# Eight experts in five runs: two experts side by side in TensorE's array, and longer rows of weights

## The chip, the cores and the metric

The kernel runs on one core of one Trainium2 chip. The metric is the device time of one execution in microseconds (us); the lower the better. The time before is 1852.3 us, the median of three runs.

## What is computed

Two layers of a hybrid transformer over 256 tokens of width 1024, in 32-bit floats. The first layer has latent attention, an RWKV-7 recurrence and 32 small experts. The second has a pooling and convolution mixer, a dense feed-forward part, the mixer again, and then the part that the change is about: 8 experts of inner width 3584, of which each token uses two. In short:

```python
for e in range(8):
    hidden = silu(t @ w1[e]) * (t @ w3[e])       # w1, w3: 1024 x 3584
    y = y + combine[:, e:e + 1] * (hidden @ w2[e])  # w2: 3584 x 1024
```

After it come a layer norm and a gate of width 1024 times a small product, and the output is written. All weights are read from HBM once: 8 x 3 x 1024 x 3584 x 4 B = 352.3 MB for these experts.

## The kernel before, in words

The program is written out engine by engine: each engine has its own list of instructions, and semaphores order them. SP issues the DMAs of all weights into a ring of 7 places of 4096 floats per partition (2 MB each) and, for these experts, an eighth place in the space of the layer norms' parameters (`work`, in the trace `work<-in_exp_w`). The semaphore `used` counts pieces that TensorE has finished; SP waits on it before it overwrites a place (`expert_free`, line 575, and `pair_piece`, line 772, with its DMA at line 784).

The experts are sorted by how many tokens chose them. For each a number of slots is set aside: `WIDTHS` (line 514) has three groups, (128, 64, 64), (128, 64, 64) and (128, 32), filled with the experts of rank (0, 3, 4), (1, 5, 6) and (2, 7). Should an expert have more tokens than slots, a slow loop at the end does the rest; it isn't entered here. A group's work is cut into units of 1024 hidden columns, three of them and one of 512 (`PARTS`, line 517). `gather_wide`, `gather_narrow` and `gather_next` pick the tokens of the slots by a matmul with a selection matrix; `rows_of` (line 2113) multiplies by a piece of w1 or w3; `turn_wide` and `turn_narrow` transpose the hidden values, `down` (line 2150) multiplies by w2, and `group_scatter` and `last_scatter` bring the results back to the tokens, again by a matmul. On VectorE `product` (line 3061) multiplies SiLU(w1 part) by the w3 part, and `turned_copy` (line 3074) copies transposes from PSUM to SBUF; ScalarE computes SiLU (line 1265).

A wide expert (128 slots) fills TensorE's 128 columns. An expert of 64 slots uses half of them, so two halves of its own weight columns are multiplied at once, at two positions in the array (`tile_position`); one of 32 slots multiplies four quarters at once. The matmuls of wide experts stand at line 2127, those of narrow ones at line 2134; the down projections at 2168 and 2176. Within a unit the order is: wide w1, wide w3, narrow w1, wide transposes, narrow w3 (then the second narrow expert's w1 and w3), wide down, narrow transposes and down (`group_pe`, line 2103). In the last group the narrow expert's last two units come at the very end (`SCHEDULE`, line 554). A piece is 2 MB: of w1 and w3 four rows of 1024 columns (4096 B runs in HBM; 2048 B in the last unit), of w2 rows of 8192 B.

The first pieces of the first expert are sent before the router's result is known (`first`, line 786); the others wait for the semaphore step "over". After the last group SP loads the weights of the gate (line 821), and POOL the last norm's parameters (line 938).

Of the kernel before, what the change touches and what calls it, by code (L numbers as in the profile page):

```python
# [74 lines left out]
AHEAD = 7  # L75

# [101 lines left out]
def build(nc, x, positions, g_mix, w_in, g_cq, w_uq, g_ckv, w_uk, w_uv, g_qn, g_kn, g_mla_out, rw_mu, rw_w0, rw_w2,  # L178
# [4 lines left out]
    with ExitStack() as ctx:  # L183
# [150 lines left out]
        p_ga, p_sc, p_scT2 = cut(work, 0, TT, 2, P), cut(work, 512, TT, 2, P), cut(work, 1024, 2, TT, P)  # L334
        p_sw, p_swT, n2_hT = cut(work, 9760, TT, P), cut(c_sb[:, :, :].rearrange("p t n -> p (t n)"), 0, TT, P), cut(work, 9248, 4, P)

        def pair_x(widths):

            return cut(xT[:, :, :].rearrange("p k s -> p (k s)"), 0, KD, sum(widths))

        p_hs, p_hh, p_hT = cut(work, 1536, 2 * 512), cut(work, 2560, 2 * 512), cut(work, 3584, 8, P)
        p_yg, p_yn = cut(work, 4608, D), cut(work, 5632, D)
        n_hs, n_hh, n_hT = cut(work, 6656, 512), cut(work, 7168, 512), cut(work, 7680, 4, P)
# [3 lines left out]
        def rt(*shape):  # L347
# [15 lines left out]
        tables, at_rt = work, [8192]  # L363
# [3 lines left out]
        slot_of, comb_of = rt(2, E2 + 1), rt(2, E2 + 1)  # L367
        over_i = sb("over_i", [P, 1], I32)
        order_i = sb("order_i", [P, E2], I32)
# [45 lines left out]
        landed_x = sem("landed_x")  # L415
# [5 lines left out]
        w_silu, w_hid, w_hTd, w_hTs, n_silu, n_hid, n_hTd, n_hTs, p_sel, p_gath, p_xg, p_scT, p_turn, p_yg_s, p_scat, p_add = (  # L421
            sem(n) for n in ("w_silu", "w_hidden", "w_hT", "w_hTs", "n_silu", "n_hidden", "n_hT", "n_hTs", "p_sel", "p_gathered",
                             "p_xg", "p_scT", "p_turned", "p_yg", "p_scattered", "p_added"))
        p_sel_w, p_clear, p_y_last = sem("p_sel_w"), sem("p_clear"), sem("p_y_last")
# [79 lines left out]
        PLE1 = MOE0 + E2 * len(MOE)  # L504
# [5 lines left out]
        def read_moe(what, u):  # L510

            return MOE0 + MOE.index((what, u)) + 1
# [3 lines left out]
        GROUPS = len(WIDTHS)  # L516
        PARTS = [(f0, min(2 * 512, F2 - f0)) for f0 in range(0, F2, 2 * 512)]
        NU = len(PARTS)

        def members(p):  # L520
            return range(len(WIDTHS[p]))

        def in_order(p, m):

            return sum(len(WIDTHS[i]) for i in range(p)) + m

        def halves(u):
            return range(PARTS[u][1] // 512)

        def pieces_of(p):  # L530

            def of(m, u, *whats):
                return [(m, what, u, a) for what in whats for a in halves(u)]

            order = []
            for wide, narrow in SCHEDULE[p]:
                if (p, wide) == (0, 0):
                    order += of(0, 0, "w1", "w3") + of(1, 0, "w1") + of(0, 0, "w2") + of(1, 0, "w3")
                    order += of(2, 0, "w1", "w3") + of(1, 0, "w2") + of(2, 0, "w2")
                    continue  # L540
                if wide is not None:
                    order += of(0, wide, "w1", "w3")
                if narrow is not None:
                    for m in members(p)[1:]:
                        order += of(m, narrow, "w1", "w3")
                if wide is not None:
                    order += of(0, wide, "w2")
                if narrow is not None:
                    for m in members(p)[1:]:
                        order += of(m, narrow, "w2")  # L550
            return order

        together = [(u, u) for u in range(NU)]
        SCHEDULE = [together] * (GROUPS - 1) + [together[:2] + [(2, None), (3, None), (None, 2), (None, 3)]]
        SCATTER_AT, GATE_AT, PLE_AT = ((4, 5), (3, 7)), ((3, 7), (4, 5)), ((0, 1), (2, 6))

        PIECES = [pieces_of(p) for p in range(GROUPS)]
        assert sum(map(len, PIECES)) == E2 * len(MOE) and E2 * len(MOE) % (PLACES + 1) == 0

        def expert_slot(n):  # L560

            turn, at = divmod(n - MOE0, PLACES + 1)
            return (turn, None) if at == 1 else (turn, MOE0 + max(at - 1, 0))

        def expert_place(n):

            first = expert_slot(n)[1]
            return lnp.rearrange("p n d -> p (n d)") if first is None else place(first)

        def expert_landed(n):  # L570

            turn, first = expert_slot(n)
            return (landed_x, 16 * (turn + 1)) if first is None else (landed[(first + 1) % PLACES], 16 * (first // PLACES + 1 + turn))

        def expert_free(n):

            turn, first = expert_slot(n)
            if turn > 0:
                return used, n - PLACES
            return bl["dve"]("ln1 1 1") if first is None else (used, first - PLACES + 1)  # L580

        def piece_of(p, m, what, u, a):

            return MOE0 + sum(map(len, PIECES[:p])) + PIECES[p].index((m, what, u, a))

        def read_pair(p, m, what, u):

            return used, piece_of(p, m, what, u, halves(u)[-1]) + 1

        def narrow_count(p, m, u):  # L590

            return sum(NU * (len(WIDTHS[i]) - 1) for i in range(p)) + u * (len(WIDTHS[p]) - 1) + m

        def gathers(p):

            return 3 + 4 * p
# [12 lines left out]
        def _(sp):  # L609
# [162 lines left out]
            def pair_piece(n, at, what, u, a):  # L772
                f0, f = PARTS[u]
                dst = expert_place(n)
                if what == "w2":
                    src = exp_w2_2[0][at, f0 + a * 512:f0 + (a + 1) * 512, :]
                    src = src.rearrange("a (j p c) n -> p (a j) (c n)", j=2, p=P)
                    dst = dst.rearrange("p (j n) -> p j n", j=2)
                else:
                    src = (exp_w1_2 if what == "w1" else exp_w3_2)[0][at].rearrange("a (k p) f -> p (a k) f", p=P)  # L780
                    rows_k = PLACE // f
                    src = src[:, rows_k * a:rows_k * (a + 1), f0:f0 + f]
                    dst = dst.rearrange("p (k f) -> p k f", f=f)
                sp.dma_start(dst, src).then_inc(expert_landed(n)[0], 16)

            first = slice(0, 1)
            sent = [v for v in PIECES[0][:PLACES + 1] if v[0] == 0]
            for m, what, u, a in sorted(sent, key=lambda v: expert_slot(piece_of(0, *v))[1] is None):
                sp.wait_ge(*expert_free(piece_of(0, m, what, u, a)))
                pair_piece(piece_of(0, m, what, u, a), first, what, u, a)  # L790
            sp.wait_ge(*bl["dve"]("over"))
            for p in range(GROUPS):
                which = {0: first} if p == 0 else {}
                for m, what, u, a in PIECES[p]:
                    if p == 0 and (m, what, u, a) in sent:
                        continue
                    n = piece_of(p, m, what, u, a)
                    sp.wait_ge(*expert_free(n))
                    if m not in which:
                        at = in_order(p, m)  # L800
                        which[m] = ranked(order_i[0:1, at:at + 1])
                    pair_piece(n, which[m], what, u, a)

            extra2 = sp.value_load(over_i[0:1, 0:1], min_val=0, max_val=S // CAP2 - 1)
            with sp.If(extra2 > 0):

                with sp.Fori(E2, 2 * E2) as e:
                    at = ranked(order_i[0:1, bass.ds(e - E2, 1)])
                    for i, (what, u) in enumerate(MOE):
                        n = MOE0 + i  # L810
                        sp.wait_ge(used, e * len(MOE) + (n - PLACES + 1))
# [4 lines left out]
            for a in range(3):  # L816
                n = PLE1 + a
                sp.wait_ge(used, n - PLACES + 1)
                src = w_g[:, 4 * a - 4:4 * a, :] if a > 0 else ple_w_2[1].rearrange("(k p) n -> p k n", p=P)
                dst = place(n)[:, 0:src.shape[1] * D].rearrange("p (a b) -> p a b", b=D)  # L820
                sp.dma_start(dst, src).then_inc(ld_gate_w if a > 0 else ld_ple_w, 16)
# [8 lines left out]
        def _(pool):  # L830
# [98 lines left out]
            for l in range(L2):  # L929
# [14 lines left out]
        def _(act):  # L944
# [304 lines left out]
            def group_act(p):  # L1249
                widths = WIDTHS[p]  # L1250
                for wide, narrow in SCHEDULE[p]:
# [3 lines left out]
                    for m in members(p):  # L1255
                        u = narrow if m else wide
                        if u is None:
                            continue
# [1106 lines left out]
        def _(dve):  # L2365
# [780 lines left out]
            for j in (2, 3):  # L3146
                ins = dve.tensor_copy(p_yn[n * j:n * (j + 1), y * j:y * (j + 1)], ps[n * j:n * (j + 1), 6, 0:y])
                if j == 2:
                    link(ins)
# [92 lines left out]
```

## Time and profile before

| | us |
|---|---|
| median of 3 runs (1850.29 to 1853.62) | 1852.3 |
| the profiled execution, span from first to last instruction | 1847.9 |
| TensorE busy (matmuls) | 1727.2 |
| VectorE busy | 444.1 |
| ScalarE busy | 197.5 |
| DMA, queue q1 (SP's), share of 16 engines | 74.0% |

The page gives the span of the profiled execution and no other time of it. In the timeline a row is a stretch of like instructions of one line: its start and its length in us, engine, line, output and inputs, the shape and how many there were; [..] behind it is the idle time before, and what ended it. Some matmul records are missing, so counts can be a little low; each 32-bit matmul of the program is two instructions in the trace, a transpose is one. In the windows the last three numbers are the granted clock of TensorE (1.00 is full speed), the share of time in which the 16 DMA engines were busy, and GB/s.

### The profile page before, as it was taken

The page shows a single profiled execution, that of the slowest core. Times are in us where ns is not written, and L with a number is a line of the kernel's source. Part 1 is how long each engine was busy: PE and PEld are TensorE (multiplying, and loading weights), DVE is VectorE, ACT ScalarE, POOL GpSimd, SP SyncE. Part 2 cuts the span into 40 slices and gives each one's busy share as a digit, 9 for nine tenths or more (in the row PEclk, how much of TensorE's full clock was granted, in tenths as well). Part 3 has the DMA queues.
Part 4 walks back from the last instruction along what each step waited for, and adds up shares of the span by engine and source line. Part 5 has one row for each costly group of instructions (what it writes and reads, how often), then busy time and mean ns, then how long its engine had stood idle before and what let it go on. Part 6 is the DMA issues. An engine that isn't in the chain of part 4 may idle for free.

```text
span 1847.9 us, 21680 instructions
## 1 busy us (share of the span) xinstructions
PE 1727.2 (93%) x9492; PEld 914.1 (49%) x9492; DVE 444.1 (24%) x772; ACT 197.5 (11%) x332; POOL 40.4 (2%) x126
## 2 busy tenths in 40 slices
PE   8989997777999999999999999999999999999988
PEld 6679564343854444548563333354333334444443
DVE  2776531112632000037340010110101001100003
ACT  2352111111121000010210000000000000000011
POOL 4002000000000000000000000000000000000000
PEclk9999999899999999999999999999999999999999
DMA  7031659999665332452388999999999999999991
GB/s 278 4 137 73 252 240 421 422 422 405 233 237 182 137 137 68 147 205 67 141 318 337 409 417 409 417 397 409 417 409 417 409 417 397 411 413 414 408 394 41
DMA packets 136508, 548.24 MB, mean 297 GB/s; under 512 B 7585, under 2 KB 12818, under 8 KB 109282
## 3 DMA queue, kind: packets, MB, share of 16 engines
q1 hardware_dynamic: 133280, 540.67, 74.0%
q0 software_dynamic: 1664, 5.05, 0.8%
q8 instruction: 72, 1.18, 0.3%
q10 hardware_dynamic: 1474, 1.19, 0.2%
q14 instruction: 18, 0.15, 0.0%
HBM read 543.51 MB, written 1.05 MB: 295 GB/s over the span
## 4 chain that ended last, share of the span: by engine, by line
PE 74%; DMA 14%; DVE 6%; SPq 2%; ACT 1%; issue 1%; ACTq 0%; DVEq 0%
PE ps L2127 15%; PE ps L2134 10%; DMA ring<-in_w_down 7%; PE ps L2168 7%; DMA ring<-in_exp_w 6%; PE ps L2176 5%; PE ps L2010 4%; PE ps L1984 4%; PE ps L2025 4%; PE ps L1882 3%; PE ps L1835 3%; PE ps L1774 2%; PE ps L1954 2%; PE ps L1922 2%; PE ps L1665 1%; PE ps L1546 1%
## 5 line engine op out<-in xcount | busy, mean ns | idle before, releaser
L2127 PE MATMUL ps<-ring,xT 128*128 128x512 f32 x592 | 258.4, 594 | 3.5 <-DMA ring<-in_exp_w 2.6
L2134 PE MATMUL ps<-ring,xT 128*64 128x512 f32 (+3 forms) x1312 | 193.2, 480 | 3.1 <-DMA ring<-in_exp_w 3.1
L2127 PEld LDWEIGHTS ps<-ring,xT 128*128 128x128 f32 x592 | 111.3, 190 | 144.8 <-issue 138.9
L3072 DVE TENSOR_TENSOR work<-work,ps 128x512 f32<-128x512 f32 (+3 forms) x32 | 38.3, 1197 | 475.8 <-PE ps L2127 341.1
L2168 PE MATMUL ps<-ring,work 128*128 128x512 f32 x320 | 144.4, 609 | 8.0 <-DMA ring<-in_exp_w 4.5
L2134 PEld LDWEIGHTS ps<-ring,xT 128*64 128x64 f32 (+1 forms) x1312 | 73.5, 127 | 114.9 <-issue 97.4
L2168 PEld LDWEIGHTS ps<-ring,work 128*128 128x128 f32 x320 | 61.5, 195 | 87.0 <-issue 83.9
L2176 PE MATMUL ps<-ring,work 128*64 128x512 f32 (+1 forms) x576 | 96.2, 523 | 1.9 <-DVE work L3082 1.9
L1265 ACT ACTIVATE work<-ps 128x512 f32<-128x512 f32 (+3 forms) x32 | 21.1, 660 | 718.0 <-PE ps L2127 401.5
L1835 PE MATMUL ps<-xT,ring 128*128 128x256 f32 x384 | 86.3, 389 | 0.0
L1752 PE MATMUL ps<-ring,work 128*32 128x256 f32 x944 | 61.2, 414 | 20.4 <-DMA ring<-in_w_up 19.3
L1835 PEld LDWEIGHTS ps<-xT,ring 128*128 128x128 f32 x384 | 74.8, 195 | 10.7
L1984 PE MATMUL ps<-ring,work 128*128 128x512 f32 x176 | 77.6, 593 | 0.6 <-DVE work L2937 0.6
L2010 PE MATMUL ps<-ring,xT 128*128 128x512 f32 (+1 forms) x192 | 77.6, 557 | 0.2 <-ACT xT L1164 0.2
L2025 PE MATMUL ps<-ring,xT 128*128 128x512 f32 (+1 forms) x192 | 77.6, 557 | 0.0
L3082 DVE COPY work<-ps 128x512 f32<-128x512 f32 (+3 forms) x32 | 24.7, 771 | 207.0 <-PE ps L2147 157.2
L2176 PEld LDWEIGHTS ps<-ring,work 128*64 128x64 f32 (+1 forms) x576 | 32.5, 128 | 58.0 <-issue 50.7
L2879 DVE SCALAR_TENSOR_TENSOR work<-work,c_sb 128x256 f32<-128x256 f32 x120 | 58.2, 485 | 4.3
L1774 PE MATMUL ps<-ring,work 128*32 128x512 f32 x256 | 38.2, 748 | 22.0 <-DMA ring<-in_w_down 20.4
L2010 PEld LDWEIGHTS ps<-ring,xT 128*128 128x128 f32 x192 | 36.4, 190 | 40.0 <-issue 38.7
L1882 PE MATMUL ps<-ring,work 128*128 128x512 f32 x128 | 55.9, 592 | 0.0
L1752 PEld LDWEIGHTS ps<-ring,work 128*32 128x32 f32 x944 | 32.6, 118 | 46.7 <-DMA ring<-in_w_up 18.1
(540 smaller groups left out, 1674.2 us busy)
## 6 DMA issues: line engine op xcount, KB each, us to landing
ring<-in_exp_w SPq DMA_DIRECT2D x147, 2048.0 KB, 23.6
work<-in_exp_w SPq DMA_DIRECT2D x21, 2048.0 KB, 23.6
ring<-in_w_down SPq DMA_DIRECT2D x32, 1024.0 KB, 18.8
ring<-in_w_up SPq DMA_DIRECT2D x31, 1024.0 KB, 19.1
ring<-in_dense_w SPq DMA_DIRECT2D x15, 2048.0 KB, 8.1
ring<-in_w_gate SPq DMA_DIRECT2D x28, 1024.0 KB, 17.5
ring<-in_w_in SPq DMA_DIRECT2D x6, 2048.0 KB, 13.8
ring<-in_w_in SPq DMA_DIRECT2D x8, 1104.0 KB, 15.4
```

Source lines behind the costliest of these rows:

```text
L1752: ins = mm(ps[32 * j:32 * j + 32, 2, n * F1:(n + 1) * F1], xg[:, k, 32 * j:32 * j + 32], half_place(4 * n + j, it)[:, k * F1:(k + 1) * F1] ...
L1774: ins = mm(ps[32 * j:32 * j + 32, 4 + n, :], hT[:, c, 32 * j:32 * j + 32], w, start=(c == 0), stop=(c == 1), tile_position=(0, 32 * j))
L1835: ins = mm(ps[:, bank, half * S:(half + 1) * S], w[:, k, i * P:(i + 1) * P], xT[:, k, :], start=(k == 0), stop=(k == KD - 1))
L1882: ins = mm(ps[:, 4 + 2 * t + n, :], mT[:, 4 * a + k, t * P:(t + 1) * P], wo[a][:, k, n * 512:(n + 1) * 512], start=(a == 0 and k == 0), st ...
L1984: ins = mm(ps[:, 4 + 2 * t + n, :], hT[:, c, :], w[:, c, n * 512:(n + 1) * 512], start=(u == 0 and c == 0), stop=(u == len(UD) - 1 and c = ...
L2010: ins = mm(ps[:, t, 0:UD[u]], xT[:, k, t * P:(t + 1) * P], chunked(place(n1), UD[u])[:, k, :], start=(k == 0), stop=(k == KD - 1))
L2025: ins = mm(ps[:, 2, 0:UD[u]], xT[:, k, t * P:(t + 1) * P], chunked(place(n3), UD[u])[:, k, :], start=(k == 0), stop=(k == KD - 1))
L2127: ins = mm(ps[:, bank + b, :], slots_k(m, k), w[:, i, b * 512:(b + 1) * 512], start=start, stop=stop)
L2134: ins = mm(ps[n * j:n * (j + 1), bank, 0:c], slots_k(m, k), columns, start=start, stop=stop, tile_position=(0, n * j))
L2168: ins = mm(ps[:, 4 + b, :], turned[:, 4 * a + c, :], w[:, c, b * 512:(b + 1) * 512], start=(first and c == 0), stop=(final and c == 3))
L2176: ins = mm(ps[n * j:n * (j + 1), 5 + m, 0:y], turned[:, at % per, n * (at // per):n * (at // per + 1)], w[:, c, col:col + y], start=(first ...
L2879: ins = stt(yv[:, j, :], vp[:, j, tap:tap + S], cw[:, tap, j:j + 1], yv[:, j, :], ALU.mult, ALU.add)
```

## The change

The second experts' stage is written anew. There are five runs, each of 128 slots: the expert of rank 0 alone; ranks 3 and 4 (64 slots each) side by side; rank 1; ranks 5 and 6; and ranks 2 and 7 with 96 and 32 slots. The expert of rank 2 so has 96 slots instead of 128. Side by side now means that the tiles in the array belong to different experts and read different pieces of weights, with the same column numbers. The runs form teams (0, 1), (2, 3), (4). The hidden width is cut into two units of 1792 columns. In a unit a run's w1 fills PSUM banks 0 to 3 with blocks of 448 columns, and right behind it its w3 fills the same four banks, each as soon as SiLU has read it; then the team's next run; then transposes and down projection of the one run and of the other. A piece is 1.835 MB (3584 floats per partition): two rows of 1792 columns of w1 or w3 (7168 B in HBM), or 14336 B per partition of w2. There are nine places, 192 pieces instead of 168. `used` rises by two when two experts' pieces are done. Nine pieces of the first expert are sent ahead. The last scatter is four matmuls; its input comes from one ScalarE and one VectorE copy. Gate weights come in three pieces instead of two. The last norm's parameters wait for the piece in the ninth place, number 187 of 192 in order of use. Core of the diff:

```diff
-        WIDTHS = ((CAP2, SMALL, SMALL), (CAP2, SMALL, SMALL), (CAP2, SMALL // 2))
-        RANKS = ((0, 3, 4), (1, 5, 6), (2, 7))
-        PARTS = [(f0, min(2 * 512, F2 - f0)) for f0 in range(0, F2, 2 * 512)]
+RUN_F = 1792
+RUN_PIECE = 2 * RUN_F
+RUN_BLOCK = RUN_F // 4
+RUN_PLACES = 9
+        RUNS = ((0,), (1, 2), (3,), (4, 5), (6, 7))
+        TEAMS = ((0, 1), (2, 3), (4,))
+        RANKS = (0, 3, 4, 1, 5, 6, 2, 7)
+        CAPS = (CAP2, SMALL, SMALL, CAP2, SMALL, SMALL, 96, 32)
+        NU = F2 // RUN_F
...
+            for team in TEAMS:
+                for u in range(NU):
+                    for r, what in [(r, what) for r in team for what in ("w1", "w3")] + [(r, "w2") for r in team]:
+                        order += [(m, what, u, a) for a in range(4) for m in RUNS[r]]
...
+            i = SENT.index(v)
+            if i >= RUN_PLACES:
+                return used, MOE0 + (i - RUN_PLACES) + 1
+            at = PLACE_OF[v]
+            if at == RUN_PLACES - 1:
+                return bl["dve"]("ln1 1 1")
+            return used, MIX1 + (2, 2, 3, 4, 6, 6, 6, 0)[at]
...
+                if what == "w2":
+                    src = exp_w2_2[0][at, u * RUN_F:(u + 1) * RUN_F, :].rearrange("a (p c) n -> p (a c n)", p=P)
+                    src = src[:, RUN_PIECE * a:RUN_PIECE * (a + 1)]
+                else:
+                    src = (exp_w1_2 if what == "w1" else exp_w3_2)[0][at].rearrange("a (k p) f -> p (a k) f", p=P)
+                    src = src[:, 2 * a:2 * a + 2, u * RUN_F:(u + 1) * RUN_F]
...
-                        pool.wait_ge(used, MOE0 + E2 * len(MOE) - PLACES + 1)
+                        pool.wait_ge(used, MOE0 + EATEN_AT[LAST_ROWS] + 1)
...
+            def rows_piece(r, what, u, a):
+                n = len(RUNS[r])
...
+                for i in range(2):
+                    k = 2 * a + i
+                    for b in range(4):
+                        if k == 0:
+                            bank_free(r, what, u, b)
+                        for m, at, width in tiles_of(r):
+                            kw = {} if width == P else {"tile_position": (0, at)}
+                            ins = mm(ps[at:at + width, b, 0:RUN_BLOCK], run_x(r)[:, k, at:at + width],
+                                     w[m][:, i, b * RUN_BLOCK:(b + 1) * RUN_BLOCK], start=(k == 0), stop=(k == KD - 1), **kw)
+                        if k == KD - 1 and b < 3:
+                            ins.then_inc(run_rows, 1)
+                ins.then_inc(used, n)
+
+            def bank_free(r, what, u, b):
+                team, i = TEAMS[team_of(r)], RUN_AT[r, u]
+                if what == "w3":
+                    pe.wait_ge(run_silu, fourth(r, u, b))
+                elif r != team[0]:
+                    pe.wait_ge(run_hid, fourth(team[0], u, b))
+                elif i > 0:
+                    pe.wait_ge(run_hTs, 4 * (i - 1) + b + 1)
...
+            def team_pe(g):
+                team, last = TEAMS[g], g == len(TEAMS) - 1
+                for u in range(NU):
+                    for r in team:
+                        if u == 0:
+                            pe.wait_ge(run_xg, r + 1)
+                        for a in range(4):
+                            rows_piece(r, "w1", u, a)
+                            if (r, u, a) == (0, 0, 2):
+                                run_gather(1, 6)
+                        if u == 0 and r == team[0] and g > 0:
+                            team_scatter(g - 1)
+                        for a in range(4):
+                            rows_piece(r, "w3", u, a)
+                    for r in team:
...
+                        run_turned(r, u)
+                        for a in range(4):
...
+                            down_piece(r, u, a)
...
+            def team_dve(g):
...
+                    for r in team:
+                        run_product(r, u)
+                    crossing = TEAMS[g + 1] if u == NU - 1 and g + 1 < len(TEAMS) else ()
+                    for r in crossing:
+                        run_select(r, slot_of)
+                    run_copies(team[0], u)
```

## Rows read from the trace of the kernel before

**Rows 1.** The page: span, busy slices of DMA and GB/s (slices of 46.2 us)

```profile
span 1847.9 us, 21680 instructions
DMA  7031659999665332452388999999999999999991
GB/s 278 4 137 73 252 240 421 422 422 405 233 237 182 137 137 68 147 205 67 141 318 337 409 417 409 417 397 409 417 409 417 409 417 397 411 413 414 408 394 41
```

**Rows 2.** Windows of the experts' stage: TensorE clock, DMA share, GB/s are last

```profile
1010.00:1770.00 760.00, 741.70 (x2942) 313.78 (x2939) 71.61 (x87) 28.45 (x44) 0.00 (x0) 0.99 1.02 411
1440.00:1770.00 330.00, 313.13 (x1322) 140.82 (x1323) 30.69 (x37) 13.36 (x21) 0.00 (x0) 0.98 1.02 410
```

**Rows 3.** SP queue: waits for places (us, times, longest), and issue to landing

```profile
SPq L784 <- PE ps L2134: 125.4, 43, 7.5
...
ring<-in_exp_w SPq DMA_DIRECT2D x147, 2048.0 KB, 23.6
```

**Rows 4.** Windows of 10 us, same columns

```profile
1140.00:1150.00 10.00, 10.00 (x24) 4.37 (x23) 0.00 (x0) 0.14 (x1) 0.00 (x0) 1.00 1.03 410
1180.00:1190.00 10.00, 10.00 (x30) 4.10 (x27) 1.05 (x1) 0.00 (x0) 0.00 (x0) 1.00 1.02 424
1210.00:1220.00 10.00, 10.00 (x31) 4.65 (x28) 0.00 (x0) 1.47 (x3) 0.00 (x0) 1.00 1.05 387
```

**Rows 5.** Timeline of TensorE: start, us, instruction, count (wide, 64, 32, down, transposes)

```profile
1361.17 20.76 PE L2127 MATMUL ps<-ring,xT 128*128 128x512 f32 x48
1381.87 7.09 PE L2134 MATMUL ps<-ring,xT 128*64 128x512 f32 x32
1388.88 1.09 PE L2141 MATMUL ps<-ident,work 128*128 128x128 f32 x8
...
1096.82 14.00 PE L2168 MATMUL ps<-ring,work 128*128 128x512 f32 x32
...
1616.26 3.66 PE L2134 MATMUL ps<-ring,xT 128*32 128x256 f32 x64
```

**Rows 6.** Timeline of TensorE: a gather of 128 slots, a part of a scatter

```profile
961.70 3.73 PE L2068 MATMUL ps<-work,xn 128*128 128x128 f32 x32
...
1268.86 1.02 PE L2093 MATMUL ps<-work 128*128 128x512 f32 x2
```

**Rows 7.** Groups of VectorE, 1050 to 1400 us: product and turned copy

```profile
L3072 DVE TENSOR_TENSOR work<-work,ps 128x512 f32<-128x512 f32 x8 | 8.5, 1064 | 70.0 <-PE ps L2134 42.2 <-PE ps L2127 27.8
L3082 DVE COPY work<-ps 128x512 f32<-128x512 f32 x7 | 4.8, 692 | 61.5 <-PE ps L2147 59.0 <-PE ps L2141 2.5
```

**Rows 8.** Timeline at the stage's start: SP's issues, TensorE's first expert matmul

```profile
880.22 1.70 SPq L784 DMA_DIRECT2D ring<-in_exp_w  x3
...
926.18 0.88 SPq L784 DMA_DIRECT2D ring<-in_exp_w  x2
...
932.25 0.37 SPq L784 DMA_DIRECT2D work<-in_exp_w  x1
946.74 0.97 SPq L784 DMA_DIRECT2D ring<-in_exp_w  x2
...
947.86 7.13 PE L2127 MATMUL ps<-ring,xT 128*128 128x512 f32 x16 [0.79 <-DVE xT L3011]
```

**Rows 9.** Timeline of the end: parameters asked for, the last down projection

```profile
1781.19 0.53 POOL L938 DMA_DIRECT2D work<-in_ln_g  x1 [971.45 <-PE ps L2134]
...
1796.51 1.93 PE L2176 MATMUL ps<-ring,work 128*32 128x256 f32 x32 [0.39 <-DVE work L3082]
```

**Rows 10.** TensorE after waits for DMA (timeline), and granted clock (windows)

```profile
322.69 5.35 PE L1752 MATMUL ps<-ring,work 128*32 128x256 f32 x64 [3.42 <-DMA ring<-in_w_up]
345.41 3.66 PE L1752 MATMUL ps<-ring,work 128*32 128x256 f32 x64
...
1682.32 15.44 PE L2168 MATMUL ps<-ring,work 128*128 128x512 f32 x32 [3.13 <-DMA ring<-in_exp_w]
...
320.00:340.00 20.00, 13.13 (x116) 6.54 (x117) 1.60 (x4) 2.25 (x3) 0.00 (x0) 0.83 1.01 422
```

More of the change, by code:

```diff
@@ L527, in halves @@
[L527 to L533, printed above, removed]
-            order = []
[L536 to L550, printed above, removed]
-            return order
@@ L553, in build @@
[L553 to L596, printed above, removed]
+            return MOE0 + N_EATEN - E2 * len(MOE) + MOE.index((what, u)) + 1
@@ new lines, in tiles_of, with side_of, team_of, rows_in_order @@
+        def tiles_of(r):
+            out = []
+            for m, at, n in slots_of_run(r):
+                w = n if n in (P, SMALL) else 32
+                out += [(m, at + w * i, w) for i in range(n // w)]
+            return out
+        def side_of(r):
+            return TEAMS[team_of(r)].index(r)
+        def team_of(r):
+            return [r in team for team in TEAMS].index(True)
+        def rows_in_order():
+            return [(r, what, u) for team in TEAMS for u in range(NU) for r in team for what in ("w1", "w3")]
@@ new lines, in run_piece @@
+                    dst = dst.rearrange("p (k f) -> p k f", f=RUN_F)
+                sp.dma_start(dst, src).then_inc(run_landed[PLACE_OF[v]], 16)
+            for v in SENT_FIRST:
+                sp.wait_ge(*run_free(v))
+                run_piece(v, slice(0, 1))
+            sp.wait_ge(*bl["dve"]("over"))
+            for team in TEAMS:
+                members = [m for r in team for m in RUNS[r]]
+                which = {0: slice(0, 1)} if 0 in members else {}
+                for v in SENT[RUN_PLACES:]:
+                    if v[0] not in members:
+                        continue
+                    sp.wait_ge(*run_free(v))
+                    if v[0] not in which:
+                        which[v[0]] = ranked(order_i[0:1, v[0]:v[0] + 1])
+                    run_piece(v, which[v[0]])
@@ new lines, in team_act @@
+                    for r in team if u == NU - 1 else ():
+                        act.wait_ge(*eaten(r, "w2", u))
+                        s = side_of(r)
+                        if last:
+                            act.activation(x_y[s][:, 0:512], ps[:, 4 + 2 * s, :], ACT.Copy).then_inc(run_y, 1)
+                        else:
+                            act.activation(x_y[s].rearrange("p (b n) -> p b n", b=2), ps[:, 4 + 2 * s:6 + 2 * s, :],
+                                           ACT.Copy).then_inc(run_y, 1)
@@ new lines, in team_scatter @@
+            def team_scatter(g):
+                team = TEAMS[g]
+                pe.wait_ge(run_scT, team[-1] + 1)
+                pe.wait_ge(run_y, team[-1] + 1)
+                for t in range(TT):
+                    for n in range(2):
+                        for s in range(len(team)):
+                            ins = mm(ps[:, 4 + 2 * t + n, :], x_scT[:, s, t, :], x_y[s][:, n * 512:(n + 1) * 512],
+                                     start=(s == 0), stop=(s == len(team) - 1))
+                    ins.then_inc(run_scat, 1)
```

677 lines of the change are left out of this document (240 added, 437 removed).

## The prediction

> **What bounds the kernel now.** I read the page's slices first, then wider windows over the second experts' stage, then the SP queue, then TensorE's timeline. From about slice 22 to the end nearly all DMA time is taken at some 410 GB/s while TensorE also shows nine tenths [rows 1]; the reader should see that two resources look full, and ask which one yields. Between 1010 and 1770 us the transfers run at 411 GB/s with a DMA share of 1.02; TensorE is busy 741.7 of 760 us, but of its 18.3 idle us 16.9 lie after 1440 [rows 2]. The experts' weights are 8 x 3 x 1024 x 3584 x 4 B = 352.3 MB, or 857 us at 411 GB/s. TensorE is close behind with its 451584 matmul columns (below). So it is nearly a tie: the weights set the pace once the nine-tenths-full engine has worked off its early lead, and SP waits for places in the ring all along without the engines running dry [rows 3].
>
> The rate is not one number. Windows in which only w1/w3 rows of 4096 B move show 410 GB/s, those with w2 rows of 8192 B 424, those with 2048 B rows, the last unit's, 387 [rows 4]. The first experts' stage, all 8192 B rows, shows 421 and 422 in its slices 7 to 9 [rows 1]; I use 422. These lie on one line, time per byte = 2.301 + 565/row length, in ps.
>
> **The change, part by part.**
>
> *TensorE, less.* Before, 3 wide experts take 86016 columns each, 4 of 64 slots half, one of 32 a quarter: 451584. After, five runs of 86016 = 430080: the third-ranked expert's 96 slots and the eighth's 32 share one pass. 512 columns take two passes; 48 instructions stand in 20.7 us from start to start, 0.43 us a pass [rows 5]. Two 64-slot tiles, or four 32-slot ones (x64 of 256 columns in 3.6 us), cost together what one full tile costs [rows 5], so packing two experts side by side is at full rate. 882 x 0.858 = 757 us become 840 x 0.858 = 721: 36 us of matmul gone.
>
> *TensorE, moved.* A piece of a run is now 3584 columns: 6.02 us by 0.43 us a pass (448 columns by proportion). Transposes: 14 per run and unit, 140 in all, 0.13 us each [rows 5], 18 us, as many as before within 7. Gathers 3.6 us per run, the scatter of a team 8 x 0.86 = 6.9 us [rows 6]: within 3 us of before.
>
> *Waits added.* Each of the two matrices now fills banks 0 to 3. Behind a unit's last w3 stands the product on DVE, 448 columns, 0.93 us from 1.064 us for 512, block by block behind matmuls of 0.75 us; then transposes, then a copy of 0.69 us [rows 7]. The copies queue behind the products on DVE, so TensorE stands some 0.6 us per unit with two runs and 1.6 us where selections come between or the team has one run; ACT's SiLU per block is done before TensorE comes back to its bank (1.5 us later). About 6 us in all. Cover: in a stage held by transfers this waiting costs nothing; without that cover, 6 us.
>
> *Transfers, faster.* w1/w3 rows become 7168 B, w2 rows 14336 B. By the line: 420 and 427 GB/s. A piece of 1.835 MB then takes 4.37 or 4.29 us, 352.3 MB in 836 us instead of 857, 21 us less. 7168 B lies between two measured lengths; 14336 B does not. Bounds for w2: 422 GB/s as now (+3.5 us) and 427. For all pieces the far bound is today's 411 (no gain), since no row shows these strides.
> The Trainium skill (DMA: Bandwidth & Descriptors, "Where 436 GB/s comes from") says that loads from HBM are held by the HBM side at about 358 GB/s; by that rule row length would bring nothing. Rows 4 show 387 to 424 and a rate that follows the row length, so the trace disagrees.
>
> *The start.* Before, three pieces go out at 880, two at 926, one at 932, and the rest only when the order of experts is known, at 946.7 [rows 8]. After, nine pieces (16.5 MB against 12.6) can be sent ahead, but then the ring is full, and the first run is wide: TensorE frees a place every 6.02 us where a transfer takes 4.37. TensorE starts its first matmul at 948.4 (947.9 [rows 8], plus 0.5 for one copy of 1024 instead of two of 512). It frees the tenth piece at 948.4 + 9 x 6.02 + 3.6 (the gather) = 1006.2; with 2 us for wait and issue, transfers run without a gap from 1008.2, 175 pieces left. What this early throttling loses, the three extra pieces give back.
>
> *Steady state.* In a unit of a two-run team TensorE needs 144 us plus 6, 36 pieces need 156. Wide stretches (48 us for 8 pieces) build up a lead, narrow ones (48 us for 16) spend it; at most 7 or 8 of nine places hold landed data. Once, at the second team's first rows, where 6.9 us of scatter are added, I count the ring full. TensorE frees the place for piece 89 at 948.4 + 5 x 48.2 (rows of runs) + 4 x 24.1 (down) + 10.7 (gathers) + 6.9 + 9.6 (transposes and waits) + 5.4 (waits for pieces) = 1318.4, the transfers want it at 1008.2 + 71 x 4.35 = 1317; with the issue and the 1.65 us by which the next place lags, 4.6 us are lost.
>
> *The last team* is one run with two pieces per step: 6.0 us of TensorE per 8.7 us of transfer, 24 times. TensorE has 60 us of slack here, and nothing but the transfers counts.
>
> *The sum.* 1008.2 + 112 x 4.37 + 63 x 4.29 + 4.6 = 1772.5; landing 1; last pair of pieces 6.0: 1779.5. The layer norm's parameters (1 MB on POOL's queue, 1781 before [rows 9]) are now asked for when piece 187 of 192 is used, ahead of the last landings: 2.4 us if all of it goes first. Slower clock in the last step: 1.5 us (below). Last down projection ends 1783.4, against 1798.4 before [rows 9]. From there to the end 49.5 us before; after, one ACT copy of 0.6, four matmuls, two adds of 1.2 give some 0.4 less: 49.0. The gate weights, 5 MB, follow the last piece by 12 us and are needed 22 us later: hidden. Span 1832.4, against 1847.9 [rows 1]. The page gives the span alone; the median of the runs, 1852.3, stands 4.4 above it. Forecast: 1836.8 us, rounded to **1837**.
>
> **Rivals.**
> A. *Longer rows bring nothing* (the rate stays 411): 175 x 4.465 moves the end of the transfers to about 1790, TensorE's saving is hidden behind them, and the median comes to 1855: no change. For it: no row shows 14336 B or this stride. Against it: three lengths on one line, two of them at the same source stride. 10 in 100.
> By the page's 358 GB/s limit it would be this case; rows 4 speak against it.
> B. *TensorE's clock falls in the last team's waits, and it becomes the bound: slower.* Place: 24 steps with 2.7 us of waiting each. After waits of 3.1 and 3.4 us matmuls took 15.4 instead of 14.0 [rows 5] and 5.35 instead of 3.66 us, and the granted clock there was 0.83, a mix of its two levels, 1.2 and 2.4 GHz [rows 10]. At 1.2 GHz a step takes 12.0 us against 8.7, so it decides once over 45 in 100 of a step's columns run slow. At 60 in 100 a step takes 9.6 and the kernel ends 22 us later, 1859. Against: the excess in rows 10 is 1.4 to 1.7 us a time, 6.0 + 1.7 is still under 8.7, and a slowed engine has no wait left to be slowed by. 6 in 100.
> The Trainium skill (TensorE: Matmul & The Clock Gate, "HAM oscillation") tells of kernels that restart at the low clock after every wait for a transfer; by it each step is slow at its start, as rows 10 show for some waits.
> C. *A mishap-free, faster case*: w2 at 427 GB/s or more, no cost for parameters or clock, no full ring: 1837 - 2.4 - 1.5 - 4.6 = 1828. 14 in 100.
> D. *The transfers come to a stop more often than counted* (pairs free two places at a time, nine smaller places): each extra gap like the 4.6 us one adds its length; two or three give 1846. 20 in 100.
> My forecast, 1832 to 1843: 50 in 100.
> Under 0.2% a measurement of this kernel can't tell from no change, so 1848.6 to 1856.0 is "same". Faster: forecast, C, most of D: 0.83; same: A mostly, 0.09; slower: B and the far end of A, 0.08. Range 1828 to 1854: it leaves out B, and what little lies below.
>
> **What would show it.** Windows in the middle of the stage at 418 to 422 GB/s, 427 where w2 moves; if they show 410, A. TensorE waits for DMA chiefly after 1580, some 50 us, under 8 before 1500. Last down projection near 1783. A granted clock under 0.7 from 1600 to 1780 with few waits for DMA would mean B. DMA share near 0.7 from 955 to 1008, a gap near 1320, and none elsewhere; others would mean D. Waits on DVE over 10 us before 1500 would make the wait step wrong.

## The result and the profile after

| | before | after |
|---|---|---|
| median, us (7 runs each) | 1850.3 | 1839.6 |
| lowest to highest | 1842.9 to 1854.6 | 1835.3 to 1843.3 |
| ratio, 95% interval | | 0.9949 (0.9929 to 0.9969) |
| span of the profiled execution | 1847.9 | 1833.9 |

The changed kernel is faster by 0.51%. Two more comparisons gave 0.9964 (0.9945 to 0.9983) and 0.9934 (0.9911 to 0.9957). The forecast was 1837.0, in a range from 1828 to 1854. As a saving it was 15.3 us; the medians of the three comparisons differ by 10.7, 5.6 and 12.8 us.

The page after, the lines that answer to [rows 1], with TensorE's busy share:

```profile
span 1833.9 us, 22707 instructions
PE 1694.4 (92%) x9967; PEld 899.3 (49%) x9967; DVE 435.5 (24%) x778; ACT 192.2 (10%) x327; POOL 40.6 (2%) x126
...
DMA  7031659999665332361568999999999999999990
GB/s 280 4 136 75 249 238 421 422 422 406 254 240 183 138 138 69 120 235 63 210 232 288 424 423 420 420 428 419 370 425 423 419 421 427 419 422 421 421 408 29
```

TensorE has 33 us less busy time, and DMA moves some 420 GB/s where it moved 410. The windows of 10 us answer to [rows 4] (the last three numbers are the granted clock, the DMA share and GB/s):

```profile
1120.00:1130.00 10.00, 10.00 (x28) 5.09 (x27) 0.00 (x0) 2.18 (x4) 0.00 (x0) 1.00 1.01 419
...
1060.00:1070.00 10.00, 10.00 (x24) 4.37 (x23) 0.00 (x0) 0.00 (x0) 0.00 (x0) 1.00 1.00 426
...
1300.00:1310.00 10.00, 10.00 (x28) 5.07 (x27) 0.00 (x0) 0.00 (x0) 0.00 (x0) 1.00 0.96 380
1310.00:1320.00 10.00, 10.00 (x41) 4.26 (x41) 3.42 (x4) 0.00 (x0) 0.00 (x0) 1.00 0.89 311
1320.00:1330.00 10.00, 10.00 (x56) 3.81 (x54) 0.00 (x0) 0.00 (x0) 0.00 (x0) 1.00 0.90 345
```

The first row is a stretch of w1/w3 pieces, now rows of 7168 B, at 419 GB/s; 4096 B rows gave 410. The second is one of w2, rows of 14336 B, at 426. Then comes the hole that was forecast near 1320 us. In the wide windows (against [rows 2]) the mean is 419 with the hole and 422 without it:

```profile
1010.00:1770.00 760.00, 716.97 (x3672) 303.64 (x3672) 65.28 (x98) 24.30 (x41) 1.06 (x2) 0.98 1.01 419
1050.00:1300.00 250.00, 247.22 (x946) 112.99 (x944) 23.38 (x37) 8.59 (x14) 0.00 (x0) 1.00 1.01 422
1330.00:1775.00 445.00, 406.82 (x2458) 163.97 (x2454) 35.80 (x54) 13.54 (x23) 1.06 (x2) 0.97 1.01 422
```

TensorE's waits before and after 1500 us (total, times, longest):

```profile
PE ps L2069 <- DMA ring<-in_exp_w: 6.8, 4, 2.5
PE ps L2123 <- DVE work L2962: 1.3, 3, 0.8
...
PE ps L2069 <- DMA ring<-in_exp_w: 18.6, 11, 2.6
PE ps L2123 <- DMA ring<-in_exp_w: 11.8, 5, 3.8
...
PE ps L2069 <- DMA work<-in_exp_w: 2.5, 1, 2.5
```

Before 1500 it waits for pieces 6.8 us; afterwards 18.6 + 11.8 + 2.5 = 32.9. So the stage turns from a near tie into one that hangs on the transfers in its second half. The start and the end of the stage on TensorE, with two steps of the last team between them:

```profile
944.44 18.31 PE L2069 MATMUL ps<-ring,xT 128*128 128x448 f32 x48 [1.39 <-DVE xT L2924]
...
1688.45 6.22 PE L2069 MATMUL ps<-ring,xT 128*32 128x448 f32 x64 [2.55 <-DMA ring<-in_exp_w]
1697.18 7.92 PE L2069 MATMUL ps<-ring,xT 128*32 128x448 f32 x64 [2.51 <-DMA ring<-in_exp_w]
...
1778.15 8.82 PE L2123 MATMUL ps<-ring,work 128*32 128x512 f32 x56 [3.83 <-DMA ring<-in_exp_w]
...
1787.77 3.67 PE L2183 MATMUL ps<-work 128*128 128x512 f32 x8 [0.81 <-ACT work L1290]
...
1791.88 7.11 PE L2193 MATMUL ps<-ring,xT 128*128 128x512 f32 x16 [0.44 <-issue]
```

Steps start 8.7 us apart, a pair of pieces at 421 GB/s, although TensorE needs 6.2 us at full clock. The last down step begins at 1778.15 and takes 8.82 us, part of it at the lower clock; the last scatter follows at 1787.77.

**A better ruler.** Spans differ by several us between executions of one kernel, mostly ahead of the stage: the first w1 matmul of the profiled executions started anywhere from 939.0 to 951.2 us. From here on I measure the stage itself, from the start of the first w1 matmul to the start of the last scatter's final group, both from the timeline of one profile. The changed kernel gives 843.3, 844.0 and 841.3 in three profiles (mean 842.9); the kernel before gives 1799.54 - 947.86 = 851.7, in its only profile. These are its rows at the stage's end:

```profile
1799.54 3.67 PE L2099 MATMUL ps<-work 128*128 128x512 f32 x8 [1.10 <-DVE work L3147]
...
1805.90 7.11 PE L2265 MATMUL ps<-ring,xT 128*128 128x512 f32 x16 [2.69 <-issue]
```

Every other row of the table rests on one profile as well, so a difference of less than 3 us is within what the three profiles of the changed kernel show among themselves.

| kernel | first w1 matmul | last scatter | stage | against 842.9 |
|---|---|---|---|---|
| before | 947.86 | 1799.54 | 851.7 | +8.8 |
| changed (three) | 944.44, 947.15, 945.45 | 1787.77, 1791.15, 1786.79 | 842.9 | |
| rows of 3584 B | 939.02 | 1807.79 | 868.8 | +25.9 |
| rows of 1792 B | 942.17 | 1865.24 | 923.1 | +80.2 |
| two DMAs, long rows | 951.21 | 1798.70 | 847.5 | +4.6 |
| two DMAs, w2 by partitions | 944.34 | 2054.25 | 1109.9 | +267 |
| idle matmuls in the last team | 944.52 | 1784.50 | 840.0 | -2.9 |
| half bytes, changed | 942.19 | 1718.81 | 776.6 | -66.3 |
| half bytes, before | 945.82 | 1784.38 | 838.6 | -13.1 against before |
| later scatter | 941.68 | 1778.73 | 837.1 | -5.8 |
| later norm parameters | 950.45 | 1792.12 | 841.7 | -1.2 |
| all three | 947.29 | 1780.90 | 833.6 | -9.3 |

### The profile page after: what moved, and what is told of

Its sections match the earlier page's. It is cut to its first block, busy times and chain, and to the rows that moved or that the text cites. A ratio compares the mean times of both kernels' runs of the same rounds, so it can differ in the third digit from the quotient of the medians.

```text
span 1833.9 us, 22707 instructions
## 1 busy us (share of the span) xinstructions
PE 1694.4 (92%) x9967; PEld 899.3 (49%) x9967; DVE 435.5 (24%) x778; ACT 192.2 (10%) x327; POOL 40.6 (2%) x126
## 4 chain that ended last, share of the span: by engine, by line
PE 68%; DMA 21%; DVE 6%; ACT 1%; SPq 1%; issue 1%; ACTq 0%; DVEq 0%
PE ps L2069 19%; PE ps L2123 11%; DMA ring<-in_exp_w 11%; DMA ring<-in_w_down 7%; PE ps L2004 4%; PE ps L1978 4%; PE ps L2019 4%; PE ps L1876 3%; PE ps L1829 3%; PE ps L1768 2%; DMA work<-in_exp_w 2%; PE ps L1948 2%; PE ps L1916 2%; PE ps L1659 2%; PE ps L1540 1%
## 5 line engine op out<-in xcount | busy, mean ns | idle before, releaser
L2069 PE MATMUL ps<-ring,xT 128*64 128x448 f32 (+2 forms) x2336 | 483.0, 559 | 30.9 <-DMA ring<-in_exp_w 24.6
L2069 PEld LDWEIGHTS ps<-ring,xT 128*64 128x64 f32 (+2 forms) x2336 | 201.5, 141 | 301.2 <-issue 299.2
L2123 PE MATMUL ps<-ring,work 128*32 128x512 f32 (+2 forms) x966 | 225.7, 614 | 9.3 <-DMA ring<-in_exp_w 9.3
L2952 DVE TENSOR_TENSOR work<-work,ps 128x448 f32<-128x448 f32 x40 | 34.4, 924 | 504.9 <-PE ps L2069 504.9
L2123 PEld LDWEIGHTS ps<-ring,work 128*32 128x32 f32 (+2 forms) x966 | 79.1, 138 | 142.9 <-issue 142.9
L1978 PE MATMUL ps<-ring,work 128*128 128x512 f32 x176 | 77.6, 593 | 0.6 <-DVE work L2862 0.6
L2069 PE MATMUL ps<-work,xT 128*32 128x448 f32 (+2 forms) x224 | 65.3, 556 | 1.1 <-DMA ring<-in_exp_w 0.8
L2123 PE MATMUL ps<-work 128*128 128x512 f32 (+2 forms) x154 | 57.6, 630 | 4.3 <-DMA ring<-in_exp_w 2.5
L2004 PEld LDWEIGHTS ps<-ring,xT 128*128 128x128 f32 x192 | 36.4, 190 | 40.0 <-issue 38.7
L1876 PE MATMUL ps<-ring,work 128*128 128x512 f32 x128 | 55.9, 592 | 0.0
L1978 PEld LDWEIGHTS ps<-ring,work 128*128 128x128 f32 x176 | 33.4, 190 | 41.6 <-issue 40.7
L2019 PEld LDWEIGHTS ps<-ring,xT 128*128 128x128 f32 x192 | 35.5, 190 | 34.2 <-issue 33.5
## 6 DMA issues: line engine op xcount, KB each, us to landing
work<-in_exp_w SPq DMA_DIRECT2D x19, 1792.0 KB, 23.7
```

Source lines behind the costliest of these rows:

```text
L1876: ins = mm(ps[:, 4 + 2 * t + n, :], mT[:, 4 * a + k, t * P:(t + 1) * P], wo[a][:, k, n * 512:(n + 1) * 512], start=(a == 0 and k == 0), st ...
L1978: ins = mm(ps[:, 4 + 2 * t + n, :], hT[:, c, :], w[:, c, n * 512:(n + 1) * 512], start=(u == 0 and c == 0), stop=(u == len(UD) - 1 and c = ...
L2004: ins = mm(ps[:, t, 0:UD[u]], xT[:, k, t * P:(t + 1) * P], chunked(place(n1), UD[u])[:, k, :], start=(k == 0), stop=(k == KD - 1))
L2019: ins = mm(ps[:, 2, 0:UD[u]], xT[:, k, t * P:(t + 1) * P], chunked(place(n3), UD[u])[:, k, :], start=(k == 0), stop=(k == KD - 1))
L2069: ins = mm(ps[at:at + width, b, 0:RUN_BLOCK], run_x(r)[:, k, at:at + width], w[m][:, i, b * RUN_BLOCK:(b + 1) * RUN_BLOCK], start=(k == 0) ...
L2123: ins = mm(ps[at:at + width, bank + n, :], turned[:, c * P + at:c * P + at + width], w[m][:, i * 512:(i + 1) * 512], start=(u == 0 and c = ...
```

## The experiments

Two theories stood against each other. **T**: the transfers set the end, and the gain is their rate, which follows the length of the rows in HBM; what TensorE saves is hidden. **R**: TensorE sets the pace, and the gain is its 36 us of saved matmuls.

**The yardstick.** The changed kernel ran again beside both sets of timed experiments.

> The changed kernel once more, as the yardstick for the runs beside it. Both theories: 0.993 to 0.997 of the kernel before.

> The changed kernel, as the yardstick for the three runs beside it.

Measured: 0.9964 and 0.9934, medians 1839.0 and 1836.1 us.

**Shorter rows.** The same bytes, pieces, places and TensorE work; only the runs in HBM are halved.

```diff
-                sp.dma_start(dst, src).then_inc(run_landed[PLACE_OF[v]], 16)
+                for h in range(2):
+                    if what == "w2":
+                        s_h, d_h = (x.rearrange("p (i c) -> p i c", i=2)[:, :, h * 896:(h + 1) * 896] for x in (src, dst))
+                    else:
+                        s_h, d_h = src[:, :, h * 896:(h + 1) * 896], dst[:, :, h * 896:(h + 1) * 896]
+                    sp.dma_start(d_h, s_h).then_inc(run_landed[PLACE_OF[v]], 16)
```

> Each piece is fetched by two DMAs with rows of 3584 B instead of one with rows of 7168 or 14336 B. Theory T (the transfers set the end, and their rate follows the row length, time per byte = 2.301 + 565/row length ps): 407 GB/s, 175 pieces x 4.51 us instead of 760 us in all, less the 4.6 us for which the ring was full: about +25 us on the changed kernel, so about 1864 us, slower than the kernel before. Rival R (the gain is TensorE's 36 us of saved matmuls): the same time as the changed kernel within 3 us.

Measured: median 1863.7, ratio 1.0102 (1.0068 to 1.0135), 24.7 us above the changed kernel beside it; the stage is 25.9 longer. One window of 10 us and the whole stretch of this run:

```profile
1120.00:1130.00 10.00, 10.00 (x28) 5.11 (x27) 0.00 (x0) 1.43 (x3) 0.00 (x0) 1.00 1.03 405
...
1010.00:1770.00 760.00, 697.96 (x3512) 298.40 (x3509) 63.96 (x96) 24.25 (x41) 0.00 (x0) 0.98 1.03 405
```

405 GB/s; the line said 407. With four DMAs of 1792 B rows:

> Four DMAs per piece with rows of 1792 B. T by the line: 382 GB/s, a piece takes 4.80 us, 175 of them 840 us instead of 760, less 4.6: a span some 75 us above the changed kernel's, near 1910 us. R: no change.

Measured in one execution: span 1911.3, stage +80.2, and the rate of the line within 1 GB/s:

```profile
1100.00:1200.00 100.00, 89.08 (x330) 40.38 (x326) 3.42 (x4) 4.34 (x8) 0.00 (x0) 0.98 1.06 381
```

R expected nothing in either run and is out as the explanation of the changed kernel's pace. But more DMAs were issued too, so a control had to have as many DMAs with long rows.

**The control that failed, and what it showed.** w1 and w3 were split by their two rows, w2 into the partitions 0 to 63 and 64 to 127.

```diff
+                for h in range(2):
+                    if what == "w2":
+                        s_h, d_h = src[64 * h:64 * (h + 1), :], dst[64 * h:64 * (h + 1), :]
+                    else:
+                        s_h, d_h = src[:, h:h + 1, :], dst[:, h:h + 1, :]
```

> Control for the run with half rows: two DMAs per piece, but rows as long as in the changed kernel (w1 and w3 split by row, w2 by partitions). T: the same as the changed kernel within 3 us. If the number of DMAs and not the row length were what costs, this would be some 25 us slower as well. R: the same.

Measured: median 2102.1, ratio 1.1377 (1.1318 to 1.1436). Neither expectation came true. A window of w2 and one of w1/w3 tell why:

```profile
1120.00:1130.00 10.00, 8.20 (x28) 2.42 (x24) 0.00 (x0) 0.00 (x0) 0.00 (x0) 0.75 1.01 218
1160.00:1170.00 10.00, 10.00 (x28) 5.04 (x27) 0.00 (x0) 1.91 (x4) 0.00 (x0) 1.00 1.02 421
```

Where w1/w3 move, two DMAs per piece run at 421 GB/s, so their number costs nothing. Where w2 moves it is 218, half the rate, at a DMA share of 1.01: a transfer into 64 partitions keeps all engines' time taken and moves half the bytes. The Trainium skill (SBUF — State Buffer, "Door 1: The DMA port swizzle") says that partitions 0 to 63 reach 8 of the 16 ports and 64 to 127 the other 8; by that a DMA into either half has half the bandwidth, and the trace agrees: 218 against 426. The mended control cut w2 by columns, over all partitions:

```diff
+                        s_h, d_h = (x.rearrange("p (i c) -> p i c", i=2)[:, h:h + 1, :] for x in (src, dst))
```

> The control mended: two DMAs per piece, w1 and w3 split by row (7168 B as in the changed kernel), w2 by column halves (7168 B instead of 14336 B) over all 128 partitions. T: w1/w3 windows at 419 to 421 GB/s, w2 windows at 420 instead of 427, 63 x 0.08 = 5 us slower than the changed kernel. If the number of DMAs were what costs in the run with half rows: 25 us slower.

Measured: median 1841.1, ratio 0.9966 (0.9949 to 0.9982), stage +4.6, as expected for w2 at 7168 B. A window of w2 and one of w1/w3:

```profile
1060.00:1070.00 10.00, 10.00 (x25) 4.40 (x24) 0.00 (x0) 0.00 (x0) 0.00 (x0) 1.00 1.02 420
1160.00:1170.00 10.00, 10.00 (x56) 3.88 (x54) 0.00 (x0) 0.00 (x0) 0.00 (x0) 1.00 1.02 420
```

420 in both: w2 lost the 6 GB/s that its 14336 B rows had given. So the number of DMAs is not it, and the row length is.

**What the rest of the change is worth.** No run lengthened the rows of the kernel before and left the rest alone, so the gain isn't split by a run. The run with 3584 B rows bounds it: at 405 GB/s, with all of TensorE's saving, the stage takes 868.8 us, 17.1 more than the kernel before at 411. An estimate by proportion in time per byte, between 421 GB/s (842.9 us) and 405 (868.8), puts the changed kernel at 411 GB/s near 859 us, some 7 us above the kernel before. By that the longer rows brought the whole gain and paid for some 7 us that the other parts of the change cost.

**TensorE's slack.** In the last team, idle matmuls were put ahead of the waits for pieces, but for those of the first w1 and the first of each w2.

```diff
+            def filler(n):
+                pe.wait_ge(run_add, 1 + 2 * (len(TEAMS) - 1))
+                for _ in range(n):
+                    mm(ps[:, 6, :], ident[:, :], xn[:, 0, 0:512], start=True, stop=True)
...
+                if r == TEAMS[-1][0] and (u, what) != (0, "w1"):
+                    filler(2)
...
+                if r == TEAMS[-1][0] and a > 0:
+                    filler(2)
```

> In the last team two idle matmuls of 512 columns (1.7 us) into an unused bank stand before each of 14 steps of w1/w3 and 6 of w2 (and before the first w3 piece), some 38 us of extra work for TensorE. T: it has 2.7 us to spare in each step, so no time is lost; the engine waits less, the granted clock stays up, and the last step takes 6.1 instead of 8.9 us: 2 to 3 us faster than the changed kernel. R (TensorE sets the pace): 36 to 38 us slower.

The expectation counted 20 places; the code has 18 (12 steps of w1/w3 and 6 of w2). The trace has 72 idle matmul instructions, 31 us at 0.43 us each, so R's figure should have been near 31.

Measured: 0.9955 (0.9937 to 0.9974), median 1836.7 against 1839.0, so the added work lost no time. First the window from 1600 to 1785 us of the changed kernel, then that of this run:

```profile
1600.00:1785.00 185.00, 152.01 (x1314) 54.52 (x1318) 14.11 (x19) 4.95 (x9) 1.06 (x2) 0.93 1.01 421
```

```profile
1600.00:1785.00 185.00, 175.74 (x1403) 60.87 (x1404) 14.73 (x20) 6.07 (x11) 1.06 (x2) 1.00 1.01 421
```

23.7 us more busy time on the same wall, and the granted clock rises from 0.93 to 1.00, so some 7 of the 31 us of filling came back as faster matmuls. The end of this run:

```profile
1777.48 6.21 PE L2134 MATMUL ps<-ring,work 128*32 128x512 f32 x56 [2.22 <-DMA ring<-in_exp_w]
...
1784.50 3.67 PE L2194 MATMUL ps<-work 128*128 128x512 f32 x8 [0.80 <-ACT work L1290]
...
1790.81 8.80 PE L2204 MATMUL ps<-ring,xT 128*128 128x512 f32 x16 [2.64 <-issue]
```

The last step takes 6.21 us instead of 8.82, and the stage is 2.9 us shorter. But TensorE then waits 2.64 us ahead of the next matmuls, where the changed kernel waited 0.44, and they take 8.80 instead of 7.11 (the granted clock from 1790 to 1800 us is 0.83, against 1.00): in these profiles all of the gain is given back behind the stage.

**TensorE alone.** If half of each piece's bytes are fetched, the transfers are out of the way and TensorE's own time is left.

```diff
-                    src = src[:, RUN_PIECE * a:RUN_PIECE * (a + 1)]
+                    src, dst = src[:, RUN_PIECE * a:RUN_PIECE * a + RUN_F], dst[:, 0:RUN_F]
...
-                    src = src[:, 2 * a:2 * a + 2, u * RUN_F:(u + 1) * RUN_F]
-                    dst = dst.rearrange("p (k f) -> p k f", f=RUN_F)
+                    src = src[:, 2 * a:2 * a + 2, u * RUN_F:u * RUN_F + RUN_F // 2]
+                    dst = dst.rearrange("p (k f) -> p k f", f=RUN_F)[:, :, 0:RUN_F // 2]
```

> The changed kernel, but each of the second experts' pieces fetches only half of its bytes (the first half of each row), so this part of the result isn't computed; TensorE's instructions are all there. It shows TensorE's own time. T: TensorE waited 40 us for pieces and some 60 us are slack, so the last down projection starts some 55 us earlier and the span is 1770 to 1780 us. R (TensorE sets the pace): the span falls by less than 5 us.

> The same for the kernel before. T: TensorE is nearly as slow as the transfers there, so only its 11 us of waits for pieces and some 4 us of lower clock go: a span of 1828 to 1836 us. Together with the run before, TensorE's own saving by the change is then 50 to 60 us (36 us of matmuls and the waits in the last group), of which the clock on the wall shows 14.

Measured, in one execution each: spans 1764.6, 5 us below the forecast of T, and 1830.2, inside it. R is out: the span fell by 69 us. The start of the last scatter, changed and before, with half bytes:

```profile
1718.81 3.67 PE L2183 MATMUL ps<-work 128*128 128x512 f32 x8 [0.81 <-ACT work L1290]
```

```profile
1784.38 3.67 PE L2099 MATMUL ps<-work 128*128 128x512 f32 x8 [1.10 <-DVE work L3147]
```

TensorE's waits in the stage, first of the changed kernel with half bytes, then of the kernel before with half bytes, longest rows:

```profile
PE ps L2098 <- DVE work L2952: 2.5, 2, 1.3
PE ps L2123 <- DVE work L2962: 1.7, 4, 0.8
PE ps L2069 <- DVE xT L2924: 1.4, 1, 1.4
```

```profile
PE ps L2141 <- DVE work L3072: 3.3, 2, 2.1
PE ps L2168 <- DVE work L3082: 2.6, 2, 1.3
PE ps L2147 <- DVE work L3072: 2.3, 3, 1.1
PE ps L2176 <- DVE work L3082: 1.9, 4, 0.5
```

No wait for a piece is left in either. TensorE alone needs 776.6 us for the stage now and needed 838.6 before: the change saves it 62.0 us (50 to 60 were forecast), while the stage with all bytes became 8.8 us shorter. 36 of them are, by the prediction's count, the matmuls of the shared run; waits for DVE inside the stage fall from 11 to 4 us; the rest I didn't take apart. Before, 13.1 us of the stage hung on the transfers; now 66.3 do.

**The hole at 1320 us.** The first team's scatter moved behind the narrow run's w1.

```diff
-                        if u == 0 and r == team[0] and g > 0:
+                        if u == 0 and r == team[-1] and g > 0:
                             team_scatter(g - 1)
```

(On DVE the adds move behind the first product likewise.)

> The first team's scatter (7 us of TensorE) stands in the second team's first unit behind the narrow run's w1 instead of the wide run's w1. T: the ring isn't full any more, so the hole in the transfers from 1300 to 1330 us (380, 311 and 345 GB/s in the changed kernel, 5.4 us lost against 421) is gone, and the end comes 4 to 5 us earlier. R: no change, TensorE has the same work.

Measured: median 1834.6 against 1836.1 beside it, ratio 0.9926 (0.9909 to 0.9943): by the medians alone the gain isn't clear of the noise. The stage is 5.8 us shorter, and the windows show why:

```profile
1300.00:1310.00 10.00, 10.00 (x40) 4.38 (x40) 3.42 (x4) 0.00 (x0) 0.00 (x0) 1.00 1.02 420
1310.00:1320.00 10.00, 10.00 (x56) 3.74 (x52) 0.00 (x0) 0.00 (x0) 0.00 (x0) 1.00 1.01 416
1320.00:1330.00 10.00, 10.00 (x55) 3.72 (x52) 0.00 (x0) 1.64 (x4) 0.00 (x0) 1.00 1.01 421
```

420, 416 and 421 GB/s where the changed kernel had 380, 311 and 345. The instructions of TensorE are the same, in another order; R has no place for that.

**The norm's parameters.**

```diff
-                        pool.wait_ge(used, MOE0 + EATEN_AT[LAST_ROWS] + 1)
+                        pool.wait_ge(used, MOE0 + N_EATEN - 2)
```

> POOL asks for the last norm's parameters (1 MB) at piece 190 of 192 instead of 187. T: the last two pieces, which shared the engines with them, land up to 2.4 us earlier, and so much earlier ends the kernel; the parameters are still there when VectorE wants them. If the 1 MB was never in the way: no change.

Measured: median 1838.5 against 1836.1, ratio 0.9940 (0.9922 to 0.9958), no gain; the stage is 1.2 us shorter, inside the 2.7 us by which the changed kernel's three profiles differ. TensorE's last wait for a pair is 2.41 us here (T: up to 2.4 us less), while the changed kernel's profiles had 3.83, 4.32 and 2.79:

```profile
1783.41 7.91 PE L2123 MATMUL ps<-ring,work 128*32 128x512 f32 x56 [2.41 <-DMA ring<-in_exp_w]
```

By these rows the 1 MB may delay the last pair by 0.4 to 1.9 us; of the whole that can't be measured.

**All three.**

> The later scatter, the later parameters and the idle matmuls of the last team together. T: 5 + 2 + 2.5 = 9 to 10 us less than the changed kernel, near 1829 us, unless TensorE's wait behind the last scatter (0.4 us, but 2.6 in the run with idle matmuls) takes 2 of them.

Measured: median 1831.2, ratio 0.9898 (0.9877 to 0.9919), against 1836.1 and 0.9934 for the changed kernel beside it. The stage is 9.3 us shorter, as summed; at the end of the run 4.9 us are left. The caveat in the expectation came true:

```profile
1780.90 3.67 PE L2194 MATMUL ps<-work 128*128 128x512 f32 x8 [0.80 <-ACT work L1290]
1787.12 8.61 PE L2204 MATMUL ps<-ring,xT 128*128 128x512 f32 x16 [2.55 <-issue]
```

2.55 us of waiting and 8.61 instead of 7.11 us of matmuls. It is the fastest version of this study, 1.0% under the kernel before.

## Why the prediction was right

- **The bound.** "It is nearly a tie", and a last team in which "nothing but the transfers counts": shown by both runs with half bytes, 13.1 us of the stage before and 66.3 now.
- **The rate.** The line through three row lengths of [rows 4] gave 420 and 427 GB/s; in windows of 10 us most of w1/w3 ran at 416 to 421 and w2 at 423 to 432, and 405 and 381 were measured for two lengths that were set on purpose (forecast 407 and 382). It held for 14336 B, beyond the measured lengths, and for a w2 source whose partitions lie 57 KB apart. Rival A falls, and with it, for one core running alone, the 358 GB/s that the prediction cited from the Trainium skill (DMA: Bandwidth & Descriptors, "Where 436 GB/s comes from").
- **TensorE's saving is hidden.** Shown by the idle matmuls and by half bytes. The prediction said 36 us of matmuls and left the rest at "within a few us of before"; TensorE's own time fell by 62.0. This step was mis-sized, and it cost nothing, because the term doesn't enter the sum. So were TensorE's waits for pieces late in the stage: some 50 us were forecast, 32.9 measured after 1500.
- **The start.** I took 948.4 us for the first w1 matmul; it was 944.4, and from 939.0 to 951.2 in other executions. The DMA share between 950 and 1010 was 0.80 where I wrote "near 0.7", and the early throttling lasted as long as worked out.
- **The ring full near 1320.** Forecast 4.6 us. Measured (421 - 380 + 421 - 311 + 421 - 345) x 10 / 421 = 5.4; removing its cause took 5.8 off the stage.
- **Landing and last step: mis-sized.** From the first matmul to the last scatter the sum gave 835.8 us (to 1783.4, and 0.8 for the copy), measured 842.9. The last pair was to land 827.5 us after the first matmul and began to be used 833.7 after it. By the windows the engines had by then moved about 2 MB more than the experts' pieces and the parameters. By the order of issue these are most likely the gate's weights, of which SP sends the first 1.1 us behind the start of the last piece's DMA, 29 us before the last pair is used:

```profile
1748.89 0.39 SPq L840 DMA_DIRECT2D ring<-in_ple_w  x1
```

So part of the engines seem to be at the gate's weights while others still move the last pieces. I had 1 us for that; 4 to 5 fit these rows. This is inferred from bytes; no run held the gate's weights back. The parameters were sized at 2.4 us; sending them later shortened the last wait by 0.4 to 1.9. The last step took 8.8 us against 7.5: the clock cost 2.6, where I took 1.5 from [rows 10].
- **The tail** after the last down step was 46.9 us instead of 49.0, mostly because TensorE went on 0.44 us after the scatter and not 2.69. That and the earlier start cancel the two terms above, so the span came out at 1833.9 against a forecast of 1832.4. The agreement is luck: in the stage itself the sum had a gain of 851.7 - 835.8 = 15.9 us, and 8.8 came. Of the 14.0 us between the two profiled spans 3.4 lie ahead of the stage, 8.4 in it and 2.25 in the stall behind the scatter.
- **A wrong sum without effect.** All pieces at 4.37 and 4.29 us make 834 us, not 836, so 23 us less than 857, not 21; the forecast was added up from the pieces and isn't touched.
- **Rival B** is right in its mechanism and wrong in its reach: steps of the last team took 7.9 us instead of 6.2 at times, the mean clock was 0.93 there. Those steps stayed under the 8.7 us of a pair of pieces, as argued; only the last step, which nothing follows, showed on the wall. "HAM oscillation" in the Trainium skill (TensorE: Matmul & The Clock Gate), cited there, tells of a restart at the low clock after every wait, in a kernel whose waits are longer than these; here some steps restarted slow and others not. Rival D's further gaps are absent: between 1010 and 1770 the only windows under 414 GB/s are those of the hole.

## What to carry to other kernels

Where two resources both look full, take the load off one of them (half the bytes, or idle matmuls) before changing the other: here TensorE alone became 62 us faster, and the stage 9, which the faster transfers account for. Plot the rate against the length of the rows in windows in which one kind of transfer moves; longer rows were a saving that needed no new idea, and its size could be read off the old trace. Once transfers decide, TensorE's work belongs where it doesn't stop the freeing of places: moving a scatter from behind the wide run's w1 to behind the narrow run's took 5.8 us off a stage from which the whole change had taken 8.8, though less of it was left at the end of the run.

## What the runs showed that I had not expected

- A DMA into 64 partitions (0 to 63, or 64 to 127) moves 214 to 221 GB/s at a full DMA share, against 416 to 432 into 128. Splitting a load by partitions made the kernel 14% slower; splitting it by columns or rows cost nothing beyond the row length.
- After waits of 2.4 to 2.6 us a step of 6.2 us took 7.7 to 7.9 in some cases and 6.2 in others, so such a wait doesn't always cost the clock. Idle matmuls in the waits held it at 1.00 for 24 us of extra busy time.
- Ahead of the first matmuls behind the stage TensorE stands for 0.04 to 2.69 us with nothing that the profile names. It was 2.5 to 2.7 in four profiles (one of them the kernel before) and under 1.5 in the others; what decides it stayed open.
